# Two PSUM banks of their own for the rotation products, and the cached keys' transpose inside the other transposes' item

## The reference

```python
h = modulate(rmsnorm(x, p['norm_mix_g']), sh1, sc1)
q, k, v, u_rwkv, u_fnet = split(h @ w_in)            # 512 + 128 + 128 + 1152 + 256 columns
q, k = axial_rope(q), axial_rope(k)                  # latent tokens only:
#   x1*cos - x2*sin, x2*cos + x1*sin  on quarters of each 64-wide head
o_attn = latent_attention(q, k, v, k_ctx, v_ctx, sink)   # k_ctx, v_ctx: cached context keys, values
```

## Time and profile before

| | us |
|---|---|
| median of 3 runs | 1935.03 |
| lowest, highest | 1934.14, 1937.83 |
| the profiled execution, its own time | 1938.06 |
| its span, first to last instruction | 1936.3 |
| PE busy in the span | 1822.3 |
| DVE, ACT, POOL busy | 1054.6, 828.9, 329.6 |

### The profile page before, as it was taken

The page is one execution under the profiler, slowest core; times in us unless marked ns, Lnnn a source line. Parts: engine busy times, 40 slices in busy tenths (PEclk is TensorE's granted clock), DMA queues, the critical chain, the costliest instruction groups (busy, mean ns, idle before and its releaser), DMA issues. The chain is left out here.

```text
span 1936.3 us, 48610 instructions
## 1 busy us (share of the span) xinstructions
PE 1822.3 (94%) x21093; PEld 1712.9 (88%) x21093; DVE 1054.6 (54%) x2344; ACT 828.9 (43%) x1736; POOL 329.6 (17%) x218
## 2 busy tenths in 40 slices
PE   6998798989999999999999997989999999999997
PEld 5898688788989999999989885878888999999997
DVE  2432765755177374747453348575535837556563
ACT  4332564653265253434433256454425524434352
POOL 3233400010220202020222440000022030111111
PEclk8999999999999999999999998999999999999999
DMA  8763600000632323232227334000021232322311
GB/s 276 231 149 101 176 4 3 3 6 24 186 100 66 88 77 99 71 93 71 86 77 212 98 120 104 5 3 7 4 66 44 71 104 61 93 73 65 100 59 55
DMA packets 215949, 161.25 MB, mean 83 GB/s; under 512 B 21968, under 2 KB 213146, under 8 KB 215738
## 3 DMA queue, kind: packets, MB, share of 16 engines
q1 hardware_dynamic: 213818, 156.13, 27.6%
q0 software_dynamic: 1920, 2.03, 0.3%
HBM read 154.99 MB, written 3.15 MB: 82 GB/s over the span
## 5 line engine op out<-in xcount | busy, mean ns | idle before, releaser
L2336 DVE SCALAR_TENSOR_TENSOR x<-PS,mod,x 128x320 f32<-128x320 f32 (+2 forms) x240 | 90.7, 433 | 301.8 <-PE PS L970 301.8
L1005 PE MATMUL PS<-T_hi,wsplit 128*128 128x320 f32 x768 | 170.0, 309 | 0.0
L969 PE MATMUL PS<-in_hi,win 128*128 128x320 f32 x480 | 148.0, 316 | 11.6 <-ACT mix L1582 8.0
L970 PE MATMUL PS<-in_hi,win 128*128 128x320 f32 x480 | 145.1, 310 | 0.0
L758 POOL TENSOR_TENSOR SfR<-ring,SfR 128x768 fp32r<-128x768 f32 (+1 forms) x24 | 41.1, 1714 | 589.4 <-ACT SfR L1543 589.4
L1739 ACT ACTIVATE mix<-PS 128x256 f32<-128x256 f32 x240 | 92.3, 384 | 98.2 <-PE PS L1318 42.4
L969 PE MATMUL PS<-hid_hi,wsplit 128*128 128x320 f32 x440 | 133.2, 311 | 0.0
L970 PE MATMUL PS<-hid_hi,wsplit 128*128 128x320 f32 x440 | 132.5, 309 | 0.0
L1005 PEld LDWEIGHTS PS<-T_hi,wsplit 128*128 128x128 f32 x768 | 128.5, 188 | 0.0
L1005 PE MATMUL PS<-h_hi,wsplit 128*128 128x320 f32 x576 | 127.6, 309 | 0.0
L1005 PE MATMUL PS<-T_lo,wsplit 128*128 128x320 f32 x384 | 118.7, 309 | 0.0
(11 more groups left out here) (491 smaller groups left out, 5549.5 us busy)
## 6 DMA issues: line engine op xcount, KB each, us to landing
ring<-in_w_ada SPq DMA_DIRECT2D x48, 1024.0 KB, 7.2
ring<-in_ffn_w_in SPq DMA_DIRECT2D x88, 512.0 KB, 5.2
ring<-in_ffn_w_out SPq DMA_DIRECT2D x16, 768.0 KB, 4.4
ring<-in_ffn_w_out SPq DMA_DIRECT2D x16, 640.0 KB, 4.1
ring<-in_w_in SPq DMA_DIRECT2D x8, 1024.0 KB, 6.7
ring<-in_w_in SPq DMA_DIRECT2D x10, 512.0 KB, 5.8
ring<-in_w_in SPq DMA_DIRECT2D x16, 256.0 KB, 5.6
ring<-in_w_out SPq DMA_DIRECT2D x16, 256.0 KB, 6.9
```

The source lines that it names most:

```text
L969: mm(lat[:, 0:TH], w, v[:, 0:TH], start=(n == 0), stop=(n == total - 1))
L970: last = mm(cx[:, 0:TH], w, v[:, TH:T], start=(n == 0), stop=(n == total - 1))
L1005: last = mm(bank[:, 0:TH], (w_lo if p == 1 else w_hi)[:, k, :], (v_lo if p == 2 else v_hi)[:, k, :], start=(q in (A11, A12, S1_) and k == ...
L2336: last = V.scalar_tensor_tensor(x[:, m, a:b], bank[:, at:at + b - a], mod[:, gate_at + m, s:s + 1], x[:, m, a:b], MUL, ADD)
```

## The change

Three things are changed.

1. The five swaps and `ckT` leave the list of items. From `q` 0 (item 11) on the list now runs `q` 0 to `q` 3, `k`, `v`, `fn` 0, `kvT`, `fn` 1 (items 11 to 19), so these units alternate between the two pairs of banks. The list is six items shorter, so later items keep the pair that they had.
2. `swap(r)` writes bank 6 + r % 2. It raises a semaphore of its own, `swap_ps`, and DVE's read raises `swap_read`. `swap(r)` for r >= 2 waits for the read of swap r - 2, and `ada_rows(8)`, which writes bank 6 next, waits for the read of swap 4. ACT's wait for swap r - 2 is now on `swap_ps`.
3. The cached keys' transpose goes to columns 256 to 383 of the `cx` bank of `kvT`, as the seventh transpose of that item; ACT's copy of it (L1601) is now the last of that item's copies. The wait for the loaded tables (`ld_par`) stands before it as before. No matmul, copy or product is added or removed, and none changes its place in the queue of its engine.

```diff
@@ item_order
-    o += [("q", 0), ("q", 1), ("swap", 0), ("q", 2), ("swap", 1), ("q", 3), ("swap", 2),
-          ("k", 0), ("swap", 3), ("v", 0), ("swap", 4), ("fn", 0), ("kvT", 0), ("ckT", 0), ("fn", 1)]
+    o += [("q", m) for m in range(4)] + [("k", 0), ("v", 0), ("fn", 0), ("kvT", 0), ("fn", 1)]
...
+        swap_ps, swap_read = sig("swap_ps", 5), sig("swap_read", 5)
@@ tensor engine
                 def swap(r):
-                    lat, cx = begin(("swap", r))
+                    if r >= 2:
+                        e.wait_ge(swap_read.sem, swap_read.upto(l, r - 1))
                     e.wait_ge(rot_raw.sem, rot_raw.upto(l, r + 1))
-                    mm(lat[:, :], swapm, raw[:, r % 2, 0:NL], start=True, stop=True).then_inc(acc_ready(), 1)
+                    mm(ps[6 + r % 2][:, :], swapm, raw[:, r % 2, 0:NL], start=True, stop=True).then_inc(swap_ps(), 1)
...
-                tr(cx[:, 128:256], kt[:, NL:T], ident).then_inc(acc_ready(), 1)
-                lat, cx = begin(("ckT", 0))
+                tr(cx[:, 128:256], kt[:, NL:T], ident)
                 e.wait_ge(ld_par.sem, ld_par.upto(l, ld_par.per))
-                tr(lat[:, 0:128], ckv[:, 0, :], ident).then_inc(acc_ready(), 1)
+                tr(cx[:, 256:384], ckv[:, 0, :], ident).then_inc(acc_ready(), 1)
                 whole(UNIT_OF[("fn", 1)])
...
+                e.wait_ge(swap_read.sem, swap_read.upto(l, 5))
                 ada_rows(8, l)
...
-                taken(e, l, ("ckT", 0))
@@ scalar engine
-                        e.wait_ge(acc_ready.sem, acc_ready.upto(l, ITEM_AT[("swap", r - 2)] + 1))
+                        e.wait_ge(swap_ps.sem, swap_ps.upto(l, r - 1))
...
-                act(kvout[:, :], cx[:, 128:256], ACT.Copy).then_inc(free(), 1)
-                free, lat, cx = ready(("ckT", 0))
-                act(kcT[:, :], lat[:, 0:128], ACT.Copy).then_inc(free(), 1)
+                act(kvout[:, :], cx[:, 128:256], ACT.Copy)
+                act(kcT[:, :], cx[:, 256:384], ACT.Copy).then_inc(free(), 1)
@@ vector engine
-                    free, lat, cx = ready(("swap", r))
+                    e.wait_ge(swap_ps.sem, swap_ps.upto(l, r + 1))
...
-                    V.tensor_tensor(rot[:, 0:NL], lat[:, :], rope[:, 1, :], MUL).then_inc(free(), 1)
-                    taken(e, l, ("swap", r))
+                    V.tensor_tensor(rot[:, 0:NL], ps[6 + r % 2], rope[:, 1, :], MUL).then_inc(swap_read(), 1)
+                    e.wait_ge(swap_read.sem, swap_read.upto(l, r + 1))
```

## The result

| | before | after |
|---|---|---|
| median, 5 runs each on the same chip, us | 1937.83 (1934.14 to 1940.37) | 1921.65 (1918.22 to 1922.74) |
| span of the profiled execution, us | 1936.3 | 1916.4 |
| from ACT's first copy of `q` 1 to its first copy of `fn` 1, layer one / two, us | 54.15 / 54.15 | 46.88 / 46.88 |
| the rest of the span, us | 1828.0 | 1822.7 |

The ratio is 0.9918, 95% interval [0.9904, 0.9931]: 16 us faster, 13 to 19 by the interval. The forecast was 1921.9 us for the changed kernel, and a gain of 13.1 us.

What follows compares the result with a forecast made beforehand. The prediction took PE to bound the kernel, with gaps where units wait for ACT's copies. Gains of 5.73 + 0.83 = 6.56 us a layer, 13.1 for two, took 1935.03 to 1921.9 us; range 1918 to 1928.

Steps and rivals of the forecast that it cites:

- What bounds: Units q 2 to fn 0: PE binds, with five gaps at unit starts, 4.9 us a layer, ended by ACT's copies.
- Part 1: Units q 2 to fn 0 alternate banks and start without waiting for the unit before: 5.73 us a layer.
- the two bounds: For the gain of alternating units, per layer: listed idle alone, 4.9 us, or from ends of units, 6.5 us.
- The upper bound of the prediction: Alternating units, measured between unit ends, 9.16 us now against 6.99 plus 0.86: 6.5 us a layer.
- Part 3: Between fn 0 and fn 1: the cached keys' transpose waits for no banks, so fn 1 starts 0.83 us sooner a layer.
- The new waits: Swaps and ada_rows(8) wait for DVE's reads, met some 14 us before a swap asks: no cost.
- The weights are not next: Split weights ready 3.5 us after a unit's end, needed at 7.85; rival that weights bind (1931 to 1935 us): 0.03.
- Carried on in full: Behind the projection, DVE's scan starts as much earlier as PE; rival that the gain is not carried: 0.05.
- The clock: At the start of attention, PE's granted clock may shift either way: +-1 us a layer, +-2 in all.
- The high end of the range: 1928 us: floors of both gains, 10.8 us, the clock's 2 us against, and a little under 2 us of run spread.
- The sum: Whole kernel: 5.73 + 0.83 = 6.56 us a layer, 13.1 us for two layers.

Runs made afterwards that it cites:

- e2_old_waits: Changed kernel in which PE again waits, after each swap, until the unit before it was copied out; 1936.17 us, ratio to before 0.9999.
- e5_copies_first: Kernel before, in which ACT copies out units q, k and v first and splits weights only then; 1928.33 us, ratio to before 0.9951.
- e8_wait_read: Changed kernel in which PE waits after each swap for DVE's read of that swap before the next unit; 1933.30 us, ratio to before 0.9985.
- e6_low_twice: Changed kernel in which POOL makes the low part of the weights of units q 2 to fn 1 twice; 1919.85 us, ratio to before 0.9914.
- e9_warm14: Changed kernel with swap 4 moved before fn 1, plus 14 unread products in PE's wait before attention; 1920.37 us, ratio to before 0.9908.
- e10: Changed kernel with swap 4 moved before fn 1, plus 6 unread products in PE's wait before attention; 1920.63 us, ratio to before 0.9911.

## Why the prediction was right

- **What bounds.** PE, and its five gaps a layer: confirmed by `e2_old_waits`, which brings them back alone, and by `e5_copies_first`, which shortens them in the old kernel.
- **Part 1, 5.73 us a layer: measured 6.44.** This term was mis-sized, low by 0.7 us a layer. The step that failed is the choice between the two bounds. I took the start that PE could have, 0.86 us after the swap, and supposed that the unit would keep its slow first matmul behind an fp32 product. The distance from the swap's start to the unit's *second* matmul was 2.28 us; with the first at 0.86 and the slow one kept it would be 1.12, and it was 1.00. The same swap stands ahead of the unit in both kernels, so that the first matmul is slow (0.42 us, and 0.26 to the second, where 0.15 is usual) comes with the wait, not with what stands ahead; `fn` 1, which still waits, still has it (0.41 and 0.26). The upper bound of the prediction, 6.5 us, counted from the ends of units, and was nearly exact.
- **Part 3, 0.83 us: measured 0.83.** The release for which the transpose waited before, L1593, is the one for which `fn` 1 now waits.
- **The new waits, nothing: measured nothing,** also with one bank. `e8_wait_read` gave the price that they don't have, 1.1 us each. DVE's additions still take 2.45 to 2.5 us beside POOL's split and its reads of the bank 0.69: the two kinds that the prediction told apart stayed apart.
- **The weights are not next:** `e6_low_twice`. In the changed kernel those of `q` 3 are ready at 142.73 and PE starts the unit at 147.34: 4.6 us of slack, where the prediction's own 7.85 - 3.5 gives 4.35; the "over five us" that it read from the earlier trace rows is too much.
- **Carried on in full:** the scan starts as much earlier as the tail ended, in both layers. In layer one it came at 190.64 and not at the forecast 194.1: 0.7 us of the difference is part 1, and 2.8 us come from ahead of the tail, which the forecast did not have.
- **The clock, +-1 us a layer.** The trace after had the lower level in the same two places, and `e9_warm14` shows what the level costs there: 0.4 to 0.5 us a layer. The prediction read its 1.0 us from PE's rows alone, while ACT sets the pace. The scatter that matters is elsewhere, in the first 140 us and in single falls of 3.4 us that wander; the rest of the span took 1822.7 to 1828.0 us in the twelve traces. The high end of the range was right to allow for it, though by the wrong place.
- **The sum.** 14.5 us by the tails, against 13.1. That the median came out within 0.3 us of the forecast is in part luck: the three runs of before that it was taken from had a median of 1935.03, and later ones 1936.3 to 1937.8.

## What to carry to other kernels

When items take turns on two sets of buffers, count where short helpers fall in the turn: a helper between each two long items puts all the long ones on one set, and each then waits for its predecessor's reader. Give the helper a buffer of its own, or let the reader free the buffer before it does other work (`e5_copies_first` had three quarters of part 1's gain with two moved lines). To size such a gap, measure from end to end of the blocks, not from the end of the wait: PE's slow first matmul goes too.

## What the runs showed that I had not expected

- Behind the fp32 swap with no wait, the unit's first matmul starts 0.45 us after the swap's start and lasts 0.71 us, so it overlaps the swap's second instruction; the second follows 1.00 us after the swap's start. After a wait the first lasts 0.42 us, with 0.26 us to the second where 0.15 is usual.
- Filling PE's wait of 8 us with idle products lifts the granted clock of the 12 us behind it from 0.79 and 0.65 to 1.00, and gains 0.4 to 0.5 us a layer, because PE then waits for ACT.
- The instructions outside the tails, the same in ten of the twelve executions (`e9` and `e10` add products there), took 1822.7 to 1828.0 us, while tails with the same waits agreed to 0.02 us. A stretch cut out of the trace tells 0.7 us with certainty where five runs can't tell 3.
